# Router logits from the plain residual in a two-layer trunk kernel: root and shift after the product, last h2 tile behind the routing, expert 2's loads in another order

## What is computed

```
x   = x + g1 * (mix @ w_out)
h2  = rms_norm(x, norm2_g) * (1 + sc2) + sh2
scores = sigmoid(h2 @ router_w)
# of 4 groups of 4 experts the group with the largest sum of its two best (scores + router_b);
# in it the two best experts, their scores scaled to sum 1
for e in range(16):
    out += gates[:, e] * ((silu(h2 @ w_gate[e]) * (h2 @ w_up[e])) @ w_down[e])
x   = x + g2 * out
```

## Time and profile before

| | us |
|---|---|
| median of 3 runs | 971.97 (971.84 to 972.64) |
| the profiled execution, its own time | 973.04 |
| its span in the trace | 971.0 |
| busy: PE, weight loads of PE, DVE, ACT, POOL | 829.7, 485.4, 407.4, 159.5, 151.4 |
| DMA, read and written | 297.27 MB and 24.28 MB, 331 GB/s over the span |

### The profile page before, as it was taken

One profiled execution on the slowest core, in us unless ns is written; L12 is line 12 of the kernel. 1 busy time (PEld: TensorE's weight loads), 2 busy tenths in 40 slices (PEclk: granted clock), 3 DMA queues, 4 the chain that ended last, 5 costly groups with the idle time before them and its releaser, 6 DMA issues.

```text
span 971.0 us, 22329 instructions
## 1 busy us (share of the span) xinstructions
PE 829.7 (85%) x8859; PEld 485.4 (50%) x8859; DVE 407.4 (42%) x893; ACT 159.5 (16%) x384; POOL 151.4 (16%) x284
## 2 busy tenths in 40 slices
PE   4699999989996889999897681999997899997674
PEld 3236644456344446658463351588653455653332
DVE  2122724566555423333232124644726655553223
ACT  3201111354012011111010012312502000000001
POOL 2302100001402334433231234000000000000000
PEclk9799999999997889999897886899997999999777
DMA  9999995860999899999999996296536899999995
GB/s 355 351 382 367 352 374 199 330 266 15 382 417 330 337 355 395 398 393 387 393 395 398 395 388 215 74 359 260 228 130 244 317 416 418 412 388 407 414 411 241
DMA packets 82359, 322.56 MB, mean 332 GB/s; under 512 B 10688, under 2 KB 28320, under 8 KB 57712
## 3 DMA queue, kind: packets, MB, share of 16 engines
q1 hardware_dynamic: 62544, 288.42, 76.3%
q0 software_dynamic: 12160, 27.89, 8.0%
q10 hardware_dynamic: 7584, 5.19, 1.8%
HBM read 297.27 MB, written 24.28 MB: 331 GB/s over the span
## 4 chain that ended last, share of the span: by engine, by line
DMA 50%; PE 40%; DVE 4%; issue 2%; ACT 2%; POOL 1%; SPq 0%; DVEq 0%; POOLq 0%; ACTq 0%
DMA weight_ring<-in_w_up_dram 22%; DMA weight_ring<-in_w_gate_dram 20%; PE bank2to L1408 9%; PE bank L1325 7%; DMA weight_ring<-in_w_mod_dram 5%; PE bank2to L1322 5%; PE bank L1322 4%; PE bank2to L1325 2%; PE bank2to L1179 2%; PE bank L1499 2%; PE bank L1357 2%; PE bank2to L1285 1%; PE bank L1374 1%; DMA weight_ring<-in_w_in_dram 1%; DMA h_by_expert<-q_k_transposed,slot_numbers 1%
## 5 line engine op out<-in xcount | busy, mean ns | idle before, releaser
L1499 PE MATMUL bank<-weight_ring,qk_tokens 128*32 128x256 f32 x3824 | 253.0, 408 | 58.1 <-DMA weight_ring<-in_w_up_dram 52.5
L1499 PEld LDWEIGHTS bank<-weight_ring,qk_tokens 128*32 128x32 f32 x3824 | 146.0, 117 | 146.5 <-issue 84.9
L898 POOL DMA_DIRECT2D qk_tokens<-h_by_expert x144 | 71.6, 497 | 161.0 <-DVE qk_tokens L2081 132.8
L1117 ACT ACTIVATE qk_tokens<-bank 64x256 f32<-64x256 f32 x62 | 23.3, 375 | 373.9 <-PE bank L1499 373.9
L1408 PE MATMUL bank2to<-weight_ring 128*128 128x512 f32 x192 | 83.7, 594 | 0.0
L2081 DVE STREAM_TRANSPOSE qk_tokens<-qk_tokens 128x256 f32<-128x256 f32 x36 | 23.9, 664 | 141.2 <-PE bank L1499 133.6
L1511 PE MATMUL bank2to<-weight_ring,qk_tokens 128*32 128x256 f32 x1280 | 79.5, 387 | 1.0 <-DVE qk_tokens L2094 1.0
L835 POOL TENSOR_SCALAR row_stats<-row_stats 128x1 f32<-128x1 f32 x22 | 4.7, 214 | 429.7 <-ACT weight_ring L1160 225.3
L2089 DVE TENSOR_TENSOR qk_tokens<-qk_tokens,bank 64x256 f32<-64x256 f32 x62 | 26.2, 423 | 103.8 <-ACT qk_tokens L1117 102.7
L1325 PE MATMUL bank<-weight_ring 128*128 128x512 f32 (+1 forms) x192 | 64.3, 489 | 0.0
L2094 DVE STREAM_TRANSPOSE qk_tokens<-qk_tokens 64x128 f32<-64x128 f32 x124 | 51.1, 412 | 28.1 <-PE bank2to L1511 26.4
(11 more groups left out here) (271 smaller groups left out, 904.5 us busy)
## 6 DMA issues: line engine op xcount, KB each, us to landing
weight_ring<-in_w_down_dram SPq DMA_DIRECT2D x64, 1024.0 KB, 7.9
weight_ring<-in_w_up_dram SPq DMA_DIRECT2D x63, 1024.0 KB, 8.3
weight_ring<-in_w_gate_dram SPq DMA_DIRECT2D x60, 1024.0 KB, 8.3
weight_ring<-in_w_mod_dram SPq DMA_DIRECT2D x24, 2048.0 KB, 10.2
weight_ring<-in_w_in_dram SPq DMA_DIRECT2D x12, 1024.0 KB, 9.0
h_by_expert<-qk_tokens POOLq DMA_DIRECT2D x17, 512.0 KB, 16.4
weight_ring<-in_w_out_dram SPq DMA_DIRECT2D x4, 2048.0 KB, 12.4
y_by_expert<-qk_tokens ACTq DMA_DIRECT2D x158, 32.0 KB, 5.8
```

Of the source, the lines that this page charges most:

```text
L898: pool.dma_start(hrow[i][q * SLOTS:(q + 1) * SLOTS, :], hsort[bass.ds((n * 2 + (AHEAD + i)) * SLOTS, SLOTS), q * Q:(q + 1) * Q]).then_inc( ...
L1117: nc.scalar.activation(sg, gate_bank(l)[0:2 * SLOTS, 0:Q], ACT.Silu).then_inc(s_si[l], 1)
L1499: mm = pe.matmul(gate_bank(l)[32 * g:32 * g + 32, 0:Q].rearrange("p (c f) -> p c f", c=2), hTe[:, k * SLOTS:(k + 1) * SLOTS], w.rearrange( ...
```

## The change

The router's product is taken from the residual instead of from h2. Since h2 = x * root * scale + shift, with scale = (1 + sc2) * norm2_g by column, the logits are root * (x @ (scale * router_w)) + shift @ router_w. So:

- SP loads sc2 and sh2 (of each stream: latent and context) and norm2_g once more, as rows of 8 x 128; PE turns them (`turn_router`), DVE makes the scaled router weights and the shift's part (`router_columns`, ahead of its part of job 2), PE sums the latter over partitions (`router_constants_row`, after job 2).
- PE turns the residual's low half of tile t after job t + 1 (`turn_low`) and its high half after job NT + t + 1 (`turn_high`); ACT copies them, DVE the last. The logits come in two halves of four matmuls; now the 128 token columns are loaded and the 16 router columns are moved, so the result lies by tokens and needs no fold.
- DVE puts root and shift to all logits at once (`scale_logits`), and ACT's sigmoid follows.
- `rows2` is split: x * scale (`rows2_scaled`) and then times root plus shift. For the last tile the second part comes behind `choose(0, SLOTS)` in layer 0 and behind `one_hot` in layer 1. PE's first pick, POOL's scatter and, in layer 1, POOL's clearing of `ysb` wait for it.
- In layer 1 scale2 and shift2 move to `qk_tokens` and `conv_y`, which frees the upper half of the up weights of expert 2's slot.
- SP loads expert 2 in another order: in layer 1 its second up half with its second gate half, before the output projection; otherwise up after expert 1's down weights, the first gate half behind the h2 of two tiles, the second down half behind the logits, and only the first down half behind the gate weights.

Diff, cut: SP and POOL

```diff
+                for s in range(NT[l] // 2):
+                    for i, part in enumerate((4, 3)):
+                        sp.dma_start(router_rows(l)[(2 * s + i) * KD:(2 * s + i + 1) * KD, :],
+                                     mod_d[l, s, part * D:(part + 1) * D].rearrange("(k p) -> k p", p=P)).then_inc(s_rc.sem, 16)
+                sp.dma_start(router_rows(l)[NT[l] * KD:(NT[l] + 1) * KD, :], norm2_g[l].rearrange("(k p) -> k p", p=P)).then_inc(s_rc.sem, 16)
...
-                    load_expert(l, 2, l + 2, GATE[1:])
+                    load_expert(l, 2, l + 2, GATE[1:] + UP[1:])
...
+                    load_expert(l, 2, l + 2, UP[:1])
+                    window.limit = 2 * MB
+                else:
+                    window.limit = 2 * MB
+                    load_expert(l, 2, l + 2, UP)
+                    sp.wait_ge(s_h2.sem, s_h2.at(l, NX))
+                    load_expert(l, 2, l + 2, GATE[:1])
+                sp.wait_ge(s_lg.sem, s_lg.at(l, NT[l]))
+                load_expert(l, 2, l + 2, DOWN[1:])
+                if early:
+                    sp.wait_ge(s_begun, 1)
+                    sp.wait_ge(s_we[(l + 2) % RING][UP[0]], weights_at(l, (l + 2) % RING, 1))
+                    load_expert(l, 2 + RING, l + 2 + RING, UP[:1])
...
-                window.limit = 2 * MB
-                load_expert(l, 2, l + 2, [i for i in range(4) if i not in early])
-                if early:
-                    sp.wait_ge(s_begun, 1)
-                    sp.wait_ge(s_we[(l + 2) % RING][UP[0]], weights_at(l, (l + 2) % RING, 1))
-                    load_expert(l, 2 + RING, l + 2 + RING, UP[:1])
+                if not early:
+                    load_expert(l, 2, l + 2, GATE[1:])
                 sp.wait_ge(s_route.sem, s_route.at(l, WEIGHTS_AT[l]))
-                load_expert(l, 2, l + 2, DOWN)
+                load_expert(l, 2, l + 2, DOWN[:1])
...
                 for t in range(NT[l]):
+                    pool.wait_ge(s_h2.sem, s_h2.at(l, t + 1))
```

```diff
+                act.wait_ge(s_rw, 32)
+                def copy_low(t):
+                    act.wait_ge(s_xp.sem, s_xp.at(l, t + 1))
+                    nc.scalar.copy(xt_low(l, t), pb[6 + t % 2][:, :]).then_inc(s_xA.sem, 1)
+                def copy_high(t):
+                    act.wait_ge(s_xp.sem, s_xp.at(l, NT[l] + t + 1))
+                    nc.scalar.copy(xt_high(l, t), pb[4 + t % 2][:, :]).then_inc(s_xA.sem, 1)
+                for t in range(NT[l]):
+                    if l == 0 and t % 2 == 0:
+                        copy_mod(LATE[t // 2])
+                    copy_low(t)
+                nc.scalar.activation(esink[:, 0:1], rbb[:, 0:1], ACT.Sigmoid)
+                for t in range(NT[l]):
+                        copy_high(t - 1)
                     act.wait_ge(s_ox.sem, s_ox.at(l, NT[l] + t + 1))
                     nc.scalar.activation(h2[:, t, :], xres[:, t, :], ACT.Square, accum_out=st[:, 2, t:t + 1]).then_inc(s_ss2.sem, 1)
+                act.wait_ge(s_rsc.sem, s_rsc.at(l, 2))
+                nc.scalar.activation(work(l, rt0, 16 * NT[l]), router_logits(l), ACT.Sigmoid).then_inc(s_sig.sem, 1)
```

```diff
+                def turn_low(t):
+                    pe.wait_ge(s_ox.sem, s_ox.at(l, t + 1))
+                    if t >= 2:
+                        pe.wait_ge(s_xA.sem, s_xA.at(l, t - 1))
+                    for k in range(HK):
+                        mm = pe.transpose(pb[6 + t % 2][:, k * P:(k + 1) * P], xres[:, t, k * P:(k + 1) * P], ident)
+                    mm.then_inc(s_xp.sem, 1)
+                def turn_high(t):
+                    pe.wait_ge(s_ox.sem, s_ox.at(l, NT[l] + t + 1))
                     if l == 0 and t == 0:
                         pe.wait_ge(s_mr, NP)
...
+                def turn_router():
+                    R = (NT[l] + 1) * KD
+                    pe.wait_ge(s_rc.sem, s_rc.at(l, 16 * (NT[l] + 2)))
+                    pe.transpose(pb[0][:, 0:R], router_rows(l)[0:R, :], ident[0:R, 0:R]).then_inc(s_rp.sem, 1)
+                def router_constants_row():
+                    pe.wait_ge(s_rsc.sem, s_rsc.at(l, 1))
+                    for s in range(NT[l] // 2):
+                        mm = pe.matmul(pb[0][:, 64 + NE * s:64 + NE * (s + 1)], rc[:, R_ONES:R_ONES + P], router_sums(l, s), start=True, stop=True)
+                    mm.then_inc(s_rp.sem, 1)
+                def logits(t, hf):
+                    if hf == 0:
+                        pe.wait_ge(s_xA.sem, s_xA.at(l, t + 1))
+                    elif t < NT[l] - 1:
+                        pe.wait_ge(s_xA.sem, s_xA.at(l, NT[l] + t + 1))
+                    else:
+                        pe.wait_ge(s_xV.sem, s_xV.at(l, 1))
+                    turned_x = (xt_low, xt_high)[hf](l, t)
+                    for k in range(HK):
+                        mm = pe.matmul((pb[0][:, 96:160], pb[1][:, 0:64])[hf][:, t * NE:(t + 1) * NE], turned_x[:, k * P:(k + 1) * P],
+                                       router_scaled(l, t // NX)[:, hf * HK + k, :], start=(k == 0), stop=(k == HK - 1))
+                    if hf == 1:
+                        mm.then_inc(s_lg.sem, 1)
+                    elif t == NT[l] - 1:
+                        mm.then_inc(s_rp.sem, 1)
+                for n in range(2 * NT[l]):
                     out_job(n)
                     if l == 0 and n in (1, 3):
                         sum_partials(LATE[n // 2])
-                for t in range(NT[l]):
-                    out_job(NT[l] + t)
...
+                    if 1 <= n <= NT[l]:
+                        turn_low(n - 1)
+                    if n == 1:
+                        turn_router()
+                    if n == 2:
+                        router_constants_row()
+                    if 2 <= n <= NT[l] + 1:
+                        logits(n - 2, 0)
+                    if n > NT[l]:
+                        turn_high(n - NT[l] - 1)
+                    if n >= NT[l] + 2:
+                        logits(n - NT[l] - 2, 1)
+                turn_high(NT[l] - 1)
+                logits(NT[l] - 2, 1)
+                logits(NT[l] - 1, 1)
...
```

```diff
+                def rows2_scaled(t):
+                    dve.wait_ge(s_ss2.sem, s_ss2.at(l, t + 1))
+                    link(V.tensor_tensor(h2[:, t, :], xres[:, t, :], scale2(l, t // NX), ALU.mult))
                 def rows2(t):
                     dve.wait_ge(s_r2.sem, s_r2.at(l, t + 1))
-                    link(V.scalar_tensor_tensor(out=h2[:, t, :], in0=xres[:, t, :], scalar=st[:, 3, t:t + 1], in1=scale2(l, s),
-                                                op0=ALU.mult, op1=ALU.mult))
-                    V.tensor_tensor(h2[:, t, :], h2[:, t, :], shift2(l, s), ALU.add).then_inc(s_h2.sem, 1)
-                def columns2(t):
-                    dve.wait_ge(s_h2p.sem, s_h2p.at(l, 2 * t + 2))
-                    if t >= 2:
-                        dve.wait_ge(s_lq.sem, s_lq.at(l, t - 1))
-                    V.tensor_copy(hr(l, t % 2)[:, 512:1024], pb[5 + 2 * (t % 2)][:, :]).then_inc(s_h2V.sem, 1)
+                    V.scalar_tensor_tensor(out=h2[:, t, :], in0=h2[:, t, :], scalar=st[:, 3, t:t + 1], in1=shift2(l, t // NX),
+                                           op0=ALU.mult, op1=ALU.add).then_inc(s_h2.sem, 1)
+                def copy_high(t):
+                    dve.wait_ge(s_xp.sem, s_xp.at(l, NT[l] + t + 1))
+                    V.tensor_copy(xt_high(l, t), pb[4 + t % 2][:, :]).then_inc(s_xV.sem, 1)
+                def router_columns():
+                    col = lambda i: router_cols(l)[:, i * KD:(i + 1) * KD]
+                    each = lambda ap: ap.unsqueeze(2).broadcast_to([P, KD, NE])
+                    g = col(NT[l])
+                    dve.wait_ge(s_rp.sem, s_rp.at(l, 1))
+                    link(V.tensor_copy(router_cols(l)[:, 0:(NT[l] + 1) * KD], pb[0][:, 0:(NT[l] + 1) * KD]))
+                    dve.wait_ge(s_rw, 32)
+                    shifted = router_rows(l).rearrange("p (k n) -> p k n", k=KD)
+                    for s in range(NT[l] // 2):
+                        link(V.scalar_tensor_tensor(out=col(2 * s), in0=col(2 * s), scalar=1.0, in1=g, op0=ALU.add, op1=ALU.mult))
+                        link(V.tensor_tensor(router_scaled(l, s), rwb[:, :, :], each(col(2 * s)), ALU.mult))
+                        link(V.tensor_tensor(shifted, rwb[:, :, :], each(col(2 * s + 1)), ALU.mult))
+                        ins = V.tensor_reduce(router_sums(l, s), shifted.rearrange("p k n -> p n k"), AX, ALU.add)
+                    ins.then_inc(s_rsc.sem, 1)
+                def copy_low_logits():
+                    n = 32 + NT[l] * NE
+                    dve.wait_ge(s_rp.sem, s_rp.at(l, 3))
+                    link(V.tensor_copy(router_low(l)[:, 0:n], pb[0][:, 64:64 + n]))
+                def scale_logits():
+                    dve.wait_ge(s_lg.sem, s_lg.at(l, NT[l]))
+                    n = NT[l] * NE
+                    link(V.tensor_tensor(router_logits(l), pb[1][:, 0:n], router_low(l)[:, 32:32 + n], ALU.add))
```

(21 more changed lines are left out.)

115 lines of the change are left out of this document (38 added, 77 removed).

## The result

| | before | after |
|---|---|---|
| median, us | 971.90 (4 runs, 971.23 to 972.64) | 984.29 (4 runs, 982.25 to 986.40) |
| span of the profiled execution, us | 971.0 | 984.1 |

A forecast was written before the change was run, and what follows sets the result against it. PE bounds the stretch up to the last output job, DMA the two expert streams, which only move. Layer 0's +10.9 us and layer 1's -2.5 sum to +8.4 on 971.97: 980.4 us, range 975.5 to 985.5.

The forecast's parts named there:

- the term that it called decisive: Layer 0: PE stalls after job 2 for router_columns, queued on the vector engine behind the w_mod load; 7.8 us.
- PE work ahead of E, 5.9: Layer 0: added turns, logits halves and constants on the full PE, less removed work, push E 5.9 us later.
- E: End of the last output-projection job on PE in each layer; forecast for layer 0 at 313.1 us, 15.8 later.
- Stall 7.8: Layer 0, after job 2: PE waits for router_columns behind partial_sums(7) and the w_mod load; 7.8 us, bounds 5.1 to 9.
- Clock 2.1: Layer 0, behind the stall: PE's lower granted clock after idling costs 2.1 us more, bounds 1.7 to 2.5.
- E to ranking, 5.15: Layer 0, routing: the ranking starts at E + 5.15 instead of E + 11.54, gaining 6.4 us.
- Scatter +1.5: Layer 0: more of SP's loads come in at the scatter's start, adding 1.5 us (0 to 2.7).
- Layer 1, -2.5: Layer 1: 2.2 us added ahead of E, 6.0 gained to the ranking, 1.3 lost to rows2; net -2.5 us.
- Rival A: Layer 0: w_mod lands early enough that PE has no stall; 970.5 us, chance 0.10.
- B: Both layers: routing 6.4 and 4.7 us earlier, PE's additions without a price; 960.9 us, chance 0.04.
- C: Layer 0: the stopped PE also delays expert 0's up and down loads, priced at 3 us; 983.4 us, chance 0.06.

The follow-up runs named there:

- e1: Kernel after, with layer 0's router_columns made on the vector engine ahead of partial_sums(7), in its wait for w_mod; ratio to before 1.0013.
- e3: e1 plus POOL's last mod_rows stores ahead of its last root and SP's two g2 loads ahead of the ranking's end; ratio to before 1.0002.
- e9: e3 with the 16 scaled router columns as loaded weights again, 128 token columns moved, four products side by side; 966.13 us, ratio to before 0.9934.

## Why the prediction was right, and where it was off

It was right in its sign and in its range, through the term that it called decisive. By its own steps:

1. *PE work ahead of E, 5.9.* 5.3 (51.4 - 46.1 in e1, where nothing stops PE). A half takes 0.81 at full clock, not 1.0; I had taken the rows of 128 moving columns for a bound. The price of the weight load alone in the Trainium skill (TensorE: Matmul & The Clock Gate, "LDWEIGHTS (loading the stationary operand)"), which made 0.85 of it, was nearer to the measured 0.81 than my 1.0. Layer 1: 2.3 for 2.2.
2. *Stall 7.8.* 7.7, released by L1979, absent in layer 1. *Clock 2.1.* **4.3: mis-sized.** I priced one group of matmuls behind an idle stretch. Here the lower clock also caught the constants and the half, for 1.5 us more, and job 3 still paid 2.9 behind them. E came to 314.1, where the forecast had 313.1.
3. *E to ranking, 5.15.* 5.4. But the *wait for mod_rows* was missing: I moved the last root and didn't follow what POOL does behind it. Its four stores land at 326.4, 12 us after E, and before only the longer way to the ranking covered them: 1.0 us. So the scatter started 5.05 us earlier after E, not 6.4.
4. *Scatter +1.5.* **+3.1: mis-sized.** I counted the loads listed beside it (1 MB more). I should have counted what no longer fits ahead of it: the bytes between E and the scatter's end are the same 13.9 MB in both kernels. Layer 0: 17.3 - 5.05 + 3.1, less 0.5 for an earlier start of the stretch, is +14.9, against +10.9 predicted.
5. *Layer 1, -2.5.* 2.32 - 5.26 = -2.9. The ranking is at E + 5.7 (5.5 forecast), the first tile at E + 19.8 (20.7). L1958 stands on the chain as foretold.

14.9 - 2.9 = +12.0. The last 1.1 of the 13.1 between the spans (0.4 between layer 0's load 3 and layer 1's first job, the rest in layer 1's stream) has no cause that a run here shows.

That the time fell inside the range was in part luck. The clock (4.3 over a bound of 2.5) and the scatter (3.1 over 2.7) lay outside their own bounds, the wait for mod_rows had no term, and all three err to the same side; 984.29 is 1.2 us from the range's upper end.

Rival A's case, no stall, is what e1 made by another way: 973.2 for its 970.5. B falls with the 5.3 us of point 1. C's mechanism, expert weights late behind the stop, did not decide: SP was done with the loads in time and DMA stood still from 300 to 314. One link is argued and not tested: that POOL's zero stores are what stretches the load of w_mod to 17 us. No run here takes them away.

## What to carry to other kernels

Before moving work off the end of a saturated engine's run, list what the new order makes that engine wait for, on the other engines' queues; nine small operations, 2.7 us in all, behind the wait for a transfer cost 12 us here, and moving them ahead of that wait took the 12 us back. Shape a thin product so that its thin side is the loaded weights: with four products side by side, that turned an even result (e3) into one that is 0.7% faster than before (e9). Where a stage is moved ahead beside a steady stream of loads, count the bytes that no longer go before it: they come back beside it, and took 3 of 5 us here.

## What was not expected of the hardware

- After 7.7 us without work PE paid 4.3 us, after 6.3 us 3.2: more than half of the stop again. Behind the longer stop the granted clock was 0.50 from 267 to 271 us and 0.75 over the next ten.
- POOL's root of one column takes 0.55 us alone and 1.39 to 1.57 beside a 1024-column vector operation; a two-column vector operation takes 2.31 beside a POOL operation of 2.34. Giving half of rows2 to the idle POOL cost 2.85 + 2.34 us there for 1.28 on the vector engine, and the stream came 2.5 us later.
